# Recurrent chain of an RWKV-7 layer on one core: inverse and strict Gram product folded ahead of the chain, two hops a chunk for three

## What is computed

```python
def step(S, inp):
    r_t, d_t, k_t, v_t, kk_t, a_t = inp
    sa = jnp.einsum('bhvk,bhk->bhv', S, -kk_t)
    S = (S * d_t[:, :, None, :] + sa[..., None] * (kk_t * a_t)[:, :, None, :]
         + v_t[..., None] * k_t[:, :, None, :])
    return S, jnp.einsum('bhvk,bhk->bhv', S, r_t)
S, o = lax.scan(step, s0, seq)
```

## Time and profile before

| | before |
|---|---|
| median of 3 runs | 1766.89 us (1763.1 to 1768.16) |
| the profiled execution's own time | 1760.71 us |
| its span | 1758.9 us, granted clock 0.953 |
| busy PE / DVE / ACT / POOL | 1617.8 / 889.4 / 629.3 / 613.4 us |
| dense products, L779 | 63% of the chain of waits that ended last |
| SP queue in that chain | 5% |
| slots 3 to 10 of the recurrent part | 924.1 to 1235.8 us of the span |

### The profile page before, as it was taken

One profiled execution on the slowest core, in us unless ns is written; L12 is line 12 of the kernel. 1 busy time (PEld: TensorE's weight loads), 2 busy tenths in 40 slices (PEclk: granted clock), 3 DMA queues, 4 the chain that ended last, 5 costly groups with the idle time before them and its releaser, 6 DMA issues.

```text
span 1758.9 us, 44459 instructions
## 1 busy us (share of the span) xinstructions
PE 1617.8 (92%) x19218; PEld 1498.2 (85%) x19218; DVE 889.4 (51%) x1225; ACT 629.3 (36%) x1051; POOL 613.4 (35%) x322
## 2 busy tenths in 40 slices
PE   6989999999999977999878888888999999999995
PEld 6976999999999976888856666666799999999994
DVE  2156776666543237623354555543476666553233
ACT  3266333323221124333444455533343323322113
POOL 3335434434443321223332232310334444443430
PEclk9999999999999997999968999989799999999997
DMA  6610232222232223222222222210422222223221
GB/s 200 184 34 25 77 123 74 82 83 83 80 98 83 82 64 94 102 61 73 63 34 41 36 39 37 38 33 16 132 79 75 81 83 84 83 79 97 83 66 54
DMA packets 306018, 133.59 MB, mean 76 GB/s; under 512 B 119035, under 2 KB 302892, under 8 KB 305716
## 3 DMA queue, kind: packets, MB, share of 16 engines
q1 hardware_dynamic: 300850, 121.80, 25.7%
q10 hardware_dynamic: 5026, 9.70, 1.5%
HBM read 116.86 MB, written 12.64 MB: 74 GB/s over the span
## 4 chain that ended last, share of the span: by engine, by line
PE 77%; DVE 8%; issue 5%; SPq 5%; ACT 3%; DMA 1%; POOL 1%; ACTq 0%; DVEq 0%; POOLq 0%
PE ps L779 63%; SPq L554 3%; SPq L541 2%; DMA tok<-reset 1%; POOL wl L612 1%; ACT S L1654 1%; PE ps L1107 1%; PE ps L1197 1%; PE ps L1297 1%; PE ps L1027 1%; DVE xl_all L2070 1%; DVE mf L2327 1%; PE ps L1117 1%; PE ps L1302 1%; PE ps L1233 1%
## 5 line engine op out<-in xcount | busy, mean ns | idle before, releaser
L612 POOL TENSOR_TENSOR wl<-raw,wh 128x1024 fp32r<-128x1024 f32 (+1 forms) x172 | 479.8, 2790 | 780.1 <-ACT wh L1455 780.1
L779 PE MATMUL ps<-xh_all,wh 128*128 128x290 f32 (+1 forms) x2112 | 462.4, 300 | 29.0 <-DVE xl_all L2146 14.3
L779 PE MATMUL ps<-xh_all,wl 128*128 128x290 f32 (+1 forms) x2112 | 457.1, 298 | 0.0
L779 PE MATMUL ps<-xl_all,wh 128*128 128x290 f32 (+1 forms) x2112 | 456.3, 297 | 0.0
L1455 ACT CAST wh<-raw 128x1024 fp32r<-128x1024 f32 (+1 forms) x172 | 191.0, 1112 | 589.9 <-PE ps L779 581.5
L779 PEld LDWEIGHTS ps<-xh_all,wh 128*128 128x128 f32 x2112 | 344.0, 191 | 39.9 <-issue 15.9
L779 PEld LDWEIGHTS ps<-xl_all,wh 128*128 128x128 f32 x2112 | 343.3, 191 | 0.0
L779 PEld LDWEIGHTS ps<-xh_all,wl 128*128 128x128 f32 x2112 | 342.6, 191 | 0.0
L779 PE MATMUL ps<-hh,wh 128*128 128x288 f32 x704 | 148.1, 292 | 0.0
L779 PE MATMUL ps<-hl,wh 128*128 128x288 f32 x704 | 148.1, 292 | 0.0
L779 PE MATMUL ps<-hh,wl 128*128 128x288 f32 x704 | 148.1, 292 | 0.0
(11 more groups left out here) (364 smaller groups left out, 2212.5 us busy)
## 6 DMA issues: line engine op xcount, KB each, us to landing
raw<-in_ffn_w_gu SPq DMA_DIRECT2D x88, 512.0 KB, 3.7
raw<-in_ffn_w_down SPq DMA_DIRECT2D x32, 704.0 KB, 4.4
raw<-in_rwkv_w_rkv SPq DMA_DIRECT2D x24, 512.0 KB, 3.7
raw<-in_attn_w_qkv SPq DMA_DIRECT2D x24, 256.0 KB, 3.5
raw<-in_attn_w_o SPq DMA_DIRECT2D x32, 128.0 KB, 2.9
tok<-reset SPq DMA_DIRECT2D x128, 32.0 KB, 2.4
raw<-in_rwkv_w_o SPq DMA_DIRECT2D x8, 512.0 KB, 3.7
spread<-table ACTq DMA_DIRECT2D x1, 3072.0 KB, 14.9
```

What stands on the lines that cost most here:

```text
L612: nc.gpsimd.tensor_tensor(wl[:, s, 0:ph.kb, :], raw[:, s, 0:ph.kb, :], wh[:, s, 0:ph.kb, :].bitcast(F32), ALU.subtract).then_inc(raw_free, 1)
L779: out = mm(ps[:, 2 * a + b, 0:n], w[:, s, k, :], o[:, k, b, 0:n] if wide else o[:, k0 + k, t0:t0 + TH], start=(first and k == 0 and w is w ...
```

## The change

The matrix product with T is taken out of the chain and done beforehand for all chunks. In slot s, for unit a, `fold_read` multiplies the masked strict Gram product by T (ScalarE writes it back over `gr`'s third part with a minus sign), and `fold_seen` multiplies z by T (ScalarE writes it back over `zr`'s z part). For this z has to have positions on the partitions, so z too is transposed by VectorE (through `cc_s`, after b) and moved by eight more DMAs on SP into `ztok`. The chain then has `chain_sa` (z times state plus Gram product times v), `sac`, `chain_s`, `S_c`. `chain_u`, `uc` and its copy are gone, and T has one buffer where it had two. The mask of `kz` is applied as (mask - 1) times the product, with the operands of the product exchanged. All groups on TensorE, ScalarE and VectorE are put in a new order over the eight chunks.

```diff
 
-            return reset[:, PADP:PADP + SEQ] if which != 0 else cc_s[:, 0:SEQ]
+            return reset[:, PADP:PADP + SEQ] if which in (1, 2) else cc_s[:, 0:SEQ]
...
+            def turned_in(i, which, name, turned):
+
+                sp.wait_ge(ev("turned_" + name), turned)
+                if which == 3:
+                    if i >= 2:
+                        sp.wait_ge(ev("folded_mm"), seen_at(i - 1))
+                elif i >= 3:
                     sp.wait_ge(ev("outs_mm"), NCH * (i - 2))
                 src = turn_buffer(which).rearrange("p (c f n) -> p c f n", f=2, n=HB)
-                dst = tok_of(i)[:, which, :].rearrange("p (c e n) -> p c e n", e=2, n=HB)
+                dst = (ztok[:] if which == 3 else tok_of(i)[:, which, :]).rearrange("p (c e n) -> p c e n", e=2, n=HB)
                 for h in range(2):
                     for e in range(2):
...
-                    for which, name in ((2, "v"), (0, "b"), (1, "k")):
-                        turned_in(s - 1, which, name)
+                    turned_in(s - 1, 2, "v", s)
+                    turned_in(s - 1, 0, "b", turned_b_at(s - 1))
+                    if s >= 2:
+                        turned_in(s - 1, 3, "b", turned_z_at(s - 1))
+                    turned_in(s - 1, 1, "k", s)
...
                 if i >= 2:
-                    pe.wait_ge(ev("tt12"), i - 1)
+                    pe.wait_ge(ev("folded"), seen_at(i - 1))
...
             def gram_kz(i):
 
                 pe.wait_ge(ev("sig_a"), min(i + 2, UNITS))
-                if i >= 3:
-                    pe.wait_ge(ev("z"), i - 2)
+                if i >= 4:
+                    pe.wait_ge(ev("z"), i - 3)
                 for c in range(NCH):
                     for part in heads2:
-                        out = mm(ps[part, G2, tk(c)], column(kx, i, part, c), zr_of(i)[part, c, 0, :], start=True, stop=True)
+                        if i:
+                            out = mm(ps[part, G2, tk(c)], zr_of(i)[part, c, 0, :], column(kx, i, part, c), start=True, stop=True)
+                        else:
+                            out = mm(ps[part, G2, tk(c)], column(kx, i, part, c), zr_of(i)[part, c, 0, :], start=True, stop=True)
...
+            def fold_read(i):
+
+                pe.wait_ge(ev("tt"), i + 1)
+                pe.wait_ge(ev("tt12"), i)
+                pe.wait_ge(ev("kz"), i + 1)
+                for c in range(NCH):
+                    for part in heads2:
+                        out = mm(ps[part, IV, tk(c)], gr_of(i)[part, 2, tk(c)], tt_of(i)[part, c, :], start=True, stop=True)
+                out.then_inc(ev("folded_mm"), 1)
+
+            def fold_seen(i):
+
+                pe.wait_ge(ev("folded"), read_at(i))
+                pe.wait_ge(ev("tok_b"), TURNED * turned_z_at(i))
+                for c in range(NCH):
+                    for part in heads2:
+                        out = mm(ps[part, IV, tk(c)], ztok[part, tk(c)], tt_of(i)[part, c, :], start=True, stop=True)
+                out.then_inc(ev("folded_mm"), 1)
...
             def chain_ready(q):
 
-                for name in ("kz", "tt"):
-                    pe.wait_ge(ev(name), q + 2)
-                for name in ("tok_b", "tok_k", "tok_v"):
+                pe.wait_ge(ev("folded"), read_at(q + 1))
+                for name in ("tok_k", "tok_v"):
                     pe.wait_ge(ev(name), TURNED * (q + 2))
-                pe.wait_ge(ev("tt12"), q + 1)
+                pe.wait_ge(ev("tok_b"), TURNED * turned_b_at(q + 1))
...
+            def chain_sa(q, c):
+
                 if c == 0:
                     for part in heads2:
-                        out = mm(o[part], gr[part, q % 2, 2, tk(0)], tok[part, q % 2, 2, tk(0)], start=True, stop=True)
+                        out = mm(ps[part, CU, 0:HD], gr[part, q % 2, 2, tk(0)], tok[part, q % 2, 2, tk(0)], start=True, stop=True)
                 else:
+                    if c == 1:
+                        pe.wait_ge(ev("folded"), seen_at(q + 1))
                     pe.wait_ge(ev("sup"), NCH * q + c)
                     for part in heads2:
-                        out = mm(o[part], zr[part, q % 3, c, 0, :], S_c[part, c - 1, :], start=False, stop=True)
-                out.then_inc(ev("u"), 1)
+                        out = mm(ps[part, CU, 0:HD], zr[part, q % 3, c, 0, :], S_c[part, c - 1, :], start=False, stop=True)
+                out.then_inc(ev("sa"), 1)
                 if c >= 1:
                     for part in heads2:
                         mm(ps[part, OB, tk(c)], S_c[part, c - 1, :], zr[part, q % 3, c, 1, :], start=True, stop=False)
...
                 pe.wait_ge(ev("dev_sq"), g + 1)
                 pe.wait_ge(ev("sig_a"), min(g + 5, UNITS))
-                pe.wait_ge(ev("kz"), min(g + 3, UNITS))
+                pe.wait_ge(ev("kz"), min(g + 4, UNITS))
...
                 if q or c >= 2:
                     act.wait_ge(ev("outs_mm"), NCH * q + c - 1)
-                A(sac[:, c % 2, :], ps[:, CU, HD:P], ACT.Copy).then_inc(ev("sac"), 1)
+                A(sac[:, c % 2, :], ps[:, CU, 0:HD], ACT.Copy).then_inc(ev("sac"), 1)
+
+            def folded_read(i):
+
+                act.wait_ge(ev("folded_mm"), read_at(i))
+                A(gr_of(i)[:, 2, :], psb(IV), ACT.Copy, scale=-1.0).then_inc(ev("folded"), 1)
+
+            def folded_seen(i):
+
+                act.wait_ge(ev("folded_mm"), seen_at(i))
+                A(zr_of(i)[:, :, 0, :], chunks(psb(IV)), ACT.Copy).then_inc(ev("folded"), 1)
...
                     dve.wait_ge(ev("hats"), 1)
                 out = turn_buffer(which)
-                if i:
+                if which == 3:
...
 
                 dve.wait_ge(ev(name + "_mm"), i + 1)
...
+                if i and which == 2:
+                    V.scalar_tensor_tensor(chunks(gr_of(i)[:, which, :]), mask, 1.0, chunks(psb(b)), ALU.subtract, ALU.mult
+                                           ).then_inc(ev(name), 1)
+                    return
                 V.tensor_tensor(chunks(gr_of(i)[:, which, :]), chunks(psb(b)), mask, ALU.mult).then_inc(ev(name), 1)
-
```

More of the change, by code:

```diff
@@ L1191, in chain_u @@
                         mm(ps[part, OB, tk(c)], S_c[part, c - 1, :], zr[part, q % 3, c, 1, :], start=True, stop=False)
-            def chain_sa(q, c):
-                pe.wait_ge(ev("uc"), NCH * q + c + 1)
-                for part in heads2:
-                    out = mm(ps[part, CU, HD:P], tt[part, q % 2, c, :], uc[part, c % 2, :], start=True, stop=True)
-                out.then_inc(ev("sa"), 1)
                 if c == 0 and q >= 1:
@@ L2405, in bonus_terms, with turned @@
                 V.tensor_tensor(own, own, kx[:, :, SEQ:T], ALU.mult).then_inc(ev("f"), 1)
[L2407 removed]
+            def turned(i, which, name, free, count):
                 if count:
[L2410 removed]
+                    dve.wait_ge(ev(free), TURNED * count)
                 if which == 1:
```

294 lines of the change are left out of this document (155 added, 139 removed).

## The result

The changed kernel takes **1792.13 us** (median, 1790.41 to 1796.08) against 1764.99 for the kernel before on the same chip: ratio 1.0156, 95% interval 1.0129 to 1.0183. It is slower by 27 us and lies outside the predicted range of 1753 to 1781; I had forecast no change. The profiled execution has a span of 1794.3 us and its own time of 1796.08.

The account below looks back on a forecast made before the run. No engine alone was the bound, but a loop over SP, a landing, VectorE and PE. Slots 3, 4 to 8, 9 and 10 gave -2.5 + 12.4 - 4.1 - 5.2 = +0.6 us: 1767 on the median, range 1753 to 1781.

Parts of the forecast that it names:

- The new loop, slots 4 to 8: Slots 4 to 8: SP, b's landing and z's transpose set the slot, 43.2 us instead of 40.5, +12.4 us in sum.
- with 0.7 for the mask this is 3.2: VectorE's run from z's transpose through the mask of `kz`, which releases `variance`: 3.2 us, 0.7 of it the mask.
- Z: Time of z's transpose on VectorE in slots 4 to 8: 22.9 us after the slot's start S, with a 5.3 us stall.
- a loop over SP, a landing and z's transpose: Slots 4 to 8: `sout`, SP's issues up to b, a 2.2 us landing, z's transpose, then PE's tail.
- Slot 9: Follows no read of states, so b's landing does not stall VectorE: 35.0 us, a saving of 4.1.
- Slot 3: Has no `variance`; 37.7 us or so against 40.3, a saving of 2.5.
- The clock: Slots 4 to 8: the low clock behind z's stall costs 1.7 us a slot, bounded by 0 and 3.5 and more.
- The rival "slower": Half clock behind z's transpose lasts until chunk 7, another 2.3 us a slot: 1779 us, from slots of 44.3; chance 0.30.
- S + 17.6: VectorE's arrival at z's transpose in chunk 4, from PE's average of 4.4 us a chunk; S is the slot's start.
- Slots 1 and 2: Left out of the sum: k's transpose no longer blocks the levels but z's does, plus or minus 2 us.
- Slot 10: Only chain, norm and gate; without the hop 24 us, a saving of 5.2.
- 0.9 us a slot of covered work: PE's added work for the two folds less the removed products with T: +0.9 us a slot, about 36 us of work.

Follow-up runs that it names:

- e1: The changed kernel with the mask of `kz` moved one chunk up on VectorE, ahead of z's transpose: 1762.8 us, ratio 1.0019 to the kernel before.
- e9: The changed kernel with `variance`'s product moved from the end of chunk 4 to the end of chunk 5 on PE: 1778.0 us, ratio 1.0089.
- e4: As e1, with z's transpose also moved behind chunk 4's state on VectorE: 1762.6 us, ratio 1.0007.
- e6: e1 with VectorE's transposes of v and of the sample rows put behind `level_first` in chunk 0: 1764.0 us, ratio 1.0007.
- e3: The kernel before, in its own order, with the product with T and the copy `uc` left out of the chain: 1745.7 us, ratio 0.9917.
- e7: e1 with both folds cut to their first chunk, no folding for chunks 1 to 7: 1754.8 us, ratio 0.9951.

## Why the prediction was wrong

**The step that failed** is the one in "The new loop, slots 4 to 8" that starts `variance` behind z's transpose: "with 0.7 for the mask this is 3.2". I saw the shared bank G2 and priced the wait only as what follows Z, the time of z's transpose. The mask stands behind level 4 on VectorE, and that needs PE's product of level 4, which PE issues right ahead of `variance`; so PE waits for its own product to go through VectorE, in every slot and whatever z does. Measured from Z: 3.3 us in slot 8, where z's transpose stalled longest, 5.3 and 5.1 in slots 4 and 5, and 7.1, 5.9 and 6.5 in slots 6, 7 and 9, where it hardly stalled or not at all. From Z to the next slot I had 18.6 + 1.7 = 20.3 us; it is 21.3 to 25.0. Of the 29.5 us by which the forecast missed the recurrent part, 10.7 stand between Z and `variance` in slots 4 to 8. e1 shows that the mask's place decides: moved alone, it takes 24 of the 27 us back. e9 shows that the wait itself is about half of that; the other half goes with the lower clock and the issue gaps, and is not traced further.

**The path** was wrong with it. I took slots 4 to 8 for a loop over SP, a landing and z's transpose. That loop is on the chain of waits in slot 8 alone; in slots 4 to 7 the slot is as long as PE's own list with its gaps, its low clock and the wait for the mask.

**Slot 9** was taken to be free of stalls, "35.0". It is 44.3: the mask holds up `variance` there too (1.8 us), z's transpose comes at S + 20.9 and not at 17.6, and the clock in it is 0.81. **Slot 3** was to save 2.5 us and saved 0.3.

**The clock** was mis-sized: 1.7 us for one low stretch. There are ten in six slots. PE's busy time per matmul rose from 207.42 / 6768 = 30.6 ns to 226.63 / 6962 = 32.6 ns, 13 us in six slots. The rival "slower", at a chance of 0.30, had this mechanism, but behind z's transpose; its sign, slots above 44.3 us, came true for another reason.

**PE's gaps without a wait** were in no term. They had been 4.9 us in six slots, and I did not ask what a new order would make of them. They are 25.9, and e1 and e4 keep 21 to 23 of them. This also moved VectorE's arrival at chunk 4, which I put at S + 17.6 from an average chunk; it was S + 19 to 22, so that z's stall was 2.8, 2.7, 0.7, 0 and 5.3 us where I had 5.3 in each.

**Slots 1 and 2**, left at plus or minus 2, cost 4.0. e6 shows why: with v's and the sample rows' transposes behind `level_first` they take 55.6 us, against 59.8 in e1 and 55.3 in the kernel before.

**Right** were: Z, forecast at S + 22.9 and found at S + 22.1 to 22.4 in slots 4 to 6, where it waited for b's landing (in slot 7 it came at 22.4 without waiting, so there the number is luck, and in slot 8 at 25.7); the 6.3 us of SP for z's DMAs (5.2 to 6.7 by slots), by this row of the changed kernel:

```profile
1135.30 6.26 SPq L573 DMA_DIRECT2D ztok<-cc_s  x8
```

the release of `variance` by the mask; and the end of the waits for the hops. Slot 10 is right in its number, -6.4 us against -5.2, but e3 shows 2.2 us of that for the hop alone, in the old order at a clock of 0.94; the changed kernel has it at 1.00. That e1, with the mask early, comes out even (1.0019) is not what my sum said either: the hop gives 14 us (e3) and the folds take 12 (e7), where I had paid the folds with 0.9 us a slot of covered work.

## What to carry to other kernels

When an order is written anew, look for every pair of groups that share a bank, and ask whether the engine that frees it still has to go through work that the waiting engine has only just issued: such a wait comes back in every slot and no faster DMA helps it. Then price the work per slot at the clock that the idle times leave, and read PE's "issue" time as a quantity that a new order can multiply, here by five. A change that shortens a chain by moving its work elsewhere is worth the difference of the two, which two small kernels measure before the whole is rebuilt.

## What the runs showed of the hardware

- PE can stop in the middle of a group of 32x32 products, 0.6 to 1.6 us in slot 7, with no semaphore in sight, and go on 1.2 to 1.6 us after a 16 KB packet of instructions has come in (so do all 159 idle times of PE without a releaser above 0.8 us, in fourteen traces); such idle time took 21 to 28 us of six slots in the new order and 4 to 5 in the old one, for nearly the same number of matmuls (6962 and 6768).
- Work added to PE can be free or better. Of two kernels with 6 to 7 us more of it, one was faster by 0.31% (interval 0.11 to 0.51) and the other even (0.9995), both with a granted clock over the whole program that was higher by 0.005 to 0.006.
- The same product of 512 columns took 1.12 us in slots 4 to 8 of the kernel before, at a granted clock of 1.0, and 2.08 in those of e1, at 0.5.
- The executions of one unchanged kernel spread over 24 us, and the longer ones are on the whole those with the lower granted clock: 1749.5 us at 0.962, 1773.2 at 0.948.
